# Decode attention: the last eight transposes of a set of cached latents are dealt out between the value matmuls of the preceding set

## The reference, cut to what matters

```python
def mla_sample(q_lat, q_rope, ckv_new, krope_new, cache_ckv, cache_krope, page_table):
    past_ckv = cache_ckv[page_table].reshape(Bd, -1, MLA_KV_LORA)      # (8, 4096, 256)
    past_kr = cache_krope[page_table].reshape(Bd, -1, MLA_ROPE)        # (8, 4096, 32)
    s_past = jnp.einsum('bthc,bsc->bhts', q_lat, past_ckv) + jnp.einsum('bthr,bsr->bhts', q_rope, past_kr)
    s_new = jnp.einsum('bthc,bsc->bhts', q_lat, ckv_new) + jnp.einsum('bthr,bsr->bhts', q_rope, krope_new)
    ...
    p = jax.nn.softmax(s, axis=-1).astype(ckv_new.dtype)
    return (jnp.einsum('bhts,bsc->bthc', p[..., :P], past_ckv) +
            jnp.einsum('bhts,bsc->bthc', p[..., P:], ckv_new))
```

## Time and profile before

| | |
|---|---|
| median of three executions | 1638.72 us (1634.9 to 1642.35) |
| the profiled execution, its own time | 1635.87 us |
| its span from first to last instruction | 1634.1 us |
| TensorE matmuls busy | 1535.8 us (94%) |
| VectorE busy | 933.1 us (57%) |
| ScalarE busy | 667.0 us (41%) |
| GpSimd busy | 165.0 us (10%) |
| mean granted clock of TensorE | 0.973 of full speed |

### The profile page before, as it was taken

One profiled execution on the slowest core, in us unless ns is written; L12 is line 12 of the kernel. 1 busy time (PEld: TensorE's weight loads), 2 busy tenths in 40 slices (PEclk: granted clock), 3 DMA queues, 4 the chain that ended last, 5 costly groups with the idle time before them and its releaser, 6 DMA issues.

```text
span 1634.1 us, 28976 instructions
## 1 busy us (share of the span) xinstructions
PE 1535.8 (94%) x11157; PEld 1287.6 (79%) x11157; DVE 933.1 (57%) x1761; ACT 667.0 (41%) x1283; POOL 165.0 (10%) x265
## 2 busy tenths in 40 slices
PE   6999998799999988798999999999999999999994
PEld 6989997556666655465888999999999998877683
DVE  6624303555455544455568777777777765454495
ACT  2246222633456633234123555555555543332341
POOL 2100000200000024330011000000000000000030
PEclk9999998999899989999999999999999999999997
DMA  7212111110000056654123122222222237645492
GB/s 252 88 54 65 44 53 44 42 52 14 27 1 27 2 219 211 202 184 166 65 90 105 58 75 76 78 78 78 78 78 78 78 110 272 186 148 186 147 302 86
DMA packets 108805, 171.50 MB, mean 105 GB/s; under 512 B 9786, under 2 KB 75192, under 8 KB 108680
## 3 DMA queue, kind: packets, MB, share of 16 engines
q1 hardware_dynamic: 93882, 117.74, 22.8%
q0 software_dynamic: 14688, 52.43, 9.3%
q10 hardware_dynamic: 144, 0.07, 0.0%
HBM read 142.59 MB, written 27.62 MB: 104 GB/s over the span
## 4 chain that ended last, share of the span: by engine, by line
PE 68%; DVE 3%; issue 2%; ACT 1%; another core or an unknown queue 1%; DMA 0%; POOL 0%; SPq 0%; ACTq 0%; DVEq 0%; POOLq 0%
PE ps L2236 9%; PE ps L2235 9%; PE ps L2234 9%; PE ps L210 7%; PE ps L211 7%; PE ps L212 7%; PE ps L1268 4%; PE ps L1598 4%; PE ps L1619 3%; PE ps L1305 2%; PE ps L1645 2%; PE ps L1282 2%; PE ps L2758 1%; DMA f_raw<-in_w_ffn_in 0%
## 5 line engine op out<-in xcount | busy, mean ns | idle before, releaser
L2234 PE MATMUL ps<-t_hi,op_hi 128*128 128x266 f32 (+1 forms) x672 | 191.6, 285 | 2.4 <-DVE gap_hi L2458 2.4
L2236 PE MATMUL ps<-t_hi,op_lo 128*128 128x266 f32 (+1 forms) x672 | 192.2, 286 | 0.0
L2235 PE MATMUL ps<-t_lo,op_hi 128*128 128x266 f32 (+1 forms) x672 | 192.0, 286 | 0.0
L210 PE MATMUL ps<-w_hi,hT_hi 128*128 128x256 f32 (+2 forms) x504 | 142.2, 282 | 3.4 <-DVE hT_lo L324 3.4
L2234 PE MATMUL ps<-h1T_hi,op_hi 128*128 128x266 f32 x504 | 143.4, 285 | 1.0 <-DVE gap_lo L2470 1.0
L2236 PE MATMUL ps<-h1T_hi,op_lo 128*128 128x266 f32 x504 | 144.1, 286 | 0.0
L2235 PE MATMUL ps<-h1T_lo,op_hi 128*128 128x266 f32 x504 | 143.4, 285 | 0.0
L210 PE MATMUL ps<-d_hi,g_hi 128*128 128x512 f32 x352 | 140.8, 400 | 1.2 <-issue 1.2
L212 PE MATMUL ps<-w_hi,hT_lo 128*128 128x256 f32 (+2 forms) x504 | 141.5, 281 | 0.0
L211 PE MATMUL ps<-w_lo,hT_hi 128*128 128x256 f32 (+2 forms) x504 | 141.4, 281 | 0.0
L211 PE MATMUL ps<-d_lo,g_hi 128*128 128x512 f32 x352 | 138.9, 395 | 0.0
(11 more groups left out here) (351 smaller groups left out, 3473.6 us busy)
## 6 DMA issues: line engine op xcount, KB each, us to landing
d_raw<-in_w_down SPq DMA_DIRECT2D x66, 512.0 KB, 3.6
f_raw<-in_w_ffn_in SPq DMA_DIRECT2D x88, 256.0 KB, 3.4
g_res<-gap_lo SPq DMA_DIRECT2D x22, 528.0 KB, 3.6
g_raw<-g_res SPq DMA_DIRECT2D x44, 192.0 KB, 3.9
w_raw<-in_w_in SPq DMA_DIRECT2D x6, 1024.0 KB, 5.3
xs<-in_x_prompt SPq DMA_DIRECT2D x8, 512.0 KB, 4.5
h_res<-xs POOLq DMA_DIRECT2D x8, 512.0 KB, 3.0
wo_raw<-in_w_o SPq DMA_DIRECT2D x2, 2048.0 KB, 7.5
```

The costliest lines, as they stand in the source:

```text
L210: nc.tensor.matmul(out, ah, bh, start=start, stop=False)
L2234: nc.tensor.matmul(o, ah, bh, start=FIRST_IN[q] and k == 0, stop=False, skip_group_check=again)
L2235: nc.tensor.matmul(o, ah, bl, start=False, stop=False, skip_group_check=again)
L2236: last = nc.tensor.matmul(o, al, bh, start=False, stop=k == 3, skip_group_check=again)
```

## The change

Only TensorE's list is changed. `turn_set`, which issued groups 0 to 5 or groups 6 to 8, becomes `turn_blocks`, which issues any run of single transposes. Groups 0 to 5 and group 6 stay where they were, before and after the transposes of the probabilities. The eight transposes of groups 7 and 8 go into `values`: behind each four value matmuls (one block j, all four sequences) come two of the eight. Where the preceding step is that of the new tokens (k = 1 and k = 10) there are only four value matmuls in all, and the eight transposes come behind them. In steps 9 and 18 nothing is transposed and nothing changes.

```diff
@@ -1584,19 +1584,22 @@
             wait_group_out(pe, pt_base[-1] - 1)
             pe.wait_ge(o_out, N_JOBS)
 
-            def turn_set(z, part):
+            def turn_blocks(z, first, count):
+
                 slot = z % SLOTS
-                if part == 0:
+                if first == 0:
                     pe.wait_ge(set_loaded[slot], 64 * (z // SLOTS + 1))
-                for n, t in turns(z)[0:SPLIT_TURN] if part == 0 else turns(z)[SPLIT_TURN:]:
-                    if t == 8:
+                for i in range(first, first + count):
+                    n, t = turns(z)[i // 4]
+                    j = i % 4
+                    if j == 0 and t == 8:
                         pe.wait_ge(rope_packed, z + 1)
-                    if n >= TURN_BANKS:
+                    if j == 0 and n >= TURN_BANKS:
                         wait_turn_out(pe, n - TURN_BANKS)
-                    for j in range(4):
-                        src = ring_c[slot][:, t // 2, j, P * (t % 2):P * (t % 2) + P] if t < 8 else ring_p[z % 2][:, j, :, :].rearrange("p b r -> p (b r)")
-                        last = nc.tensor.transpose(ps[:, n % TURN_BANKS, P * j:P * j + P], src, ident)
-                    last.then_inc(past_turned, 1)
+                    src = ring_c[slot][:, t // 2, j, P * (t % 2):P * (t % 2) + P] if t < 8 else ring_p[z % 2][:, j, :, :].rearrange("p b r -> p (b r)")
+                    last = nc.tensor.transpose(ps[:, n % TURN_BANKS, P * j:P * j + P], src, ident)
+                    if j == 3:
+                        last.then_inc(past_turned, 1)
 
             def scores(k):
                 g, s, z = s_steps[k]
@@ -1631,8 +1634,9 @@
                         last = nc.tensor.transpose(ps[:, 6, P * j:P * j + P], sprob[k % 2][:, P * j:P * j + P], ident)
                 last.then_inc(spt_turned, 1)
 
-            def values(k):
+            def values(k, turning):
                 g, s, z = s_steps[k]
+                left = 4 * (N_TURN - SPLIT_TURN) - 4
                 pe.wait_ge(spt_out, k + 1)
                 if k >= 1:
                     pe.wait_ge(sacc_done, k)
@@ -1644,18 +1648,23 @@
                             w, x = spt[k % 2][:, j, 32 * b:32 * b + 32], ring_c[z % SLOTS][:, b, j, :]
                         last = nc.tensor.matmul(ps[32 * b:32 * b + 32, 7, 0:KVL], w, x, start=j == 0,
                                                 stop=s is None or j == 3)
-                last.then_inc(spv_done, 1)
+                    if s is None or j == 3:
+                        last.then_inc(spv_done, 1)
+                    if turning is not None:
+                        m = left if s is None else left // 4
+                        turn_blocks(turning, 4 * SPLIT_TURN + 4 + m * j, m)
 
             n = len(s_steps)
             for k in range(n + 1):
-                if k < n and s_steps[k][1] is not None:
-                    turn_set(s_steps[k][2], 0)
+                turning = s_steps[k][2] if k < n and s_steps[k][1] is not None else None
+                if turning is not None:
+                    turn_blocks(turning, 0, 4 * SPLIT_TURN)
                 if k >= 1:
                     turn_probs(k - 1)
-                if k < n and s_steps[k][1] is not None:
-                    turn_set(s_steps[k][2], 1)
+                if turning is not None:
+                    turn_blocks(turning, 4 * SPLIT_TURN, 4)
                 if k >= 1:
-                    values(k - 1)
+                    values(k - 1, turning)
                 if k < n:
                     scores(k)
         def turn_latents(pe):
```

## The result

| | before | after |
|---|---|---|
| median | 1640.53 us (1634.9 to 1645.55, 4 runs) | 1672.53 us (1666.23 to 1677.52, 4 runs) |
| the profiled execution, its own time | 1635.87 us | 1666.23 us |
| its span | 1634.1 us | 1664.4 us |
| the stage, first scores of the new tokens to first matmul of the output projection | 188.6 us | 223.4 us |

The ratio of the times is 1.0194, with a 95% interval of 1.0144 to 1.0244: slower, by 32 us in the medians; whether by 2% or somewhat less the interval leaves open. The stage grew by 34.9 us; the rest of this one profiled execution was 4.6 us shorter, which is within the 11 us by which the runs of either kernel differ among themselves.

A forecast was written before the change was run, and what follows sets the result against it. The prediction took TensorE to bound the kernel: 14 steps x 2.83 = 39.6 us, less 1.4, 1.2 and 1.5, plus 2.1, gave +37.6 on 1635.87, thus 1673.5; it forecast a median of 1675 us, range 1656 to 1693.

The forecast's parts named there:

- Changes of shape: TensorE switching between transpose and value tile shapes: 0.28 us a round trip, four more per step, 1.13 us.
- the 0.16 that was borrowed: Going out from 128x32 values to whole-array transposes: 0.16 us, taken from the change from 32x32 to transposes.
- The first rival: Shape changes between values and transposes are free, transpose loads running under value passes: 1.82 us per step, 1661 us; chance 0.12.
- The new wait: Scores wait for VectorE's copy of group 8: start 1.06 us after the last transpose, 0.83 of it new.
- Values to scores: Stretch from first value matmul to scores in a regular step: from 1.75 to 4.58 us, 2.83 more, in 14 steps.
- What the first part gives back: Values start earlier with eight transposes fewer ahead: 0.48 us gained in three steps (1.4 in all), zero in eleven.
- the third rival: Lateness reaches the scores' notice: VectorE's maximum 1.4 us late in eleven steps, +15 us, 1690 us; chance 0.10.
- Single steps: Sets differing from the regular step: 4, 11, 12 together -1.2 us; set 5 -1.5; set 0 costs 1.1, set 8 1.0.
- The clock: Rival: TensorE's granted clock falls to 1.2 GHz for part of each step, 28 us more, 1703 us; chance 0.04.

## Why the prediction came out right, point by point

The forecast was 1675 us and the median is 1672.5; the stage grew by 34.9 us against 37.6. That the two medians lie so close is partly luck. The forecast counted from a median of 1638.72, and with the fourth execution that of before is 1640.53: the medians grew by 32.0 us, where the forecast meant 36.3. Its own sum would give 1676.3 (1635.87 + 37.6 + 2.85), and 1675 was written without a reason. Errors of the terms also went against each other; they are added up below the list. By the steps of the sum:

- **Changes of shape**: predicted 0.28 us a round trip, measured 0.285 and 0.29. Out of the values it is 0.57 us from the start of a run of eight passes to the first transpose and 0.36 from there back; the 0.16 that was borrowed from the change between two other shapes held. The first rival (free shapes, 0.65 us from run to run) is refuted by 0.94. The Trainium skill, "TensorEngine Tiling (Array Packing)", Key Properties, says that changing the tiling mode drains TensorE; these 0.29 us agree with it. The Trainium skill, "TensorE: Matmul & The Clock Gate", Part 2, says that the reorder window pulls weight loads ahead of matmuls in flight; across a change of shape the 0.94 us show no gain from it.
- **The new wait**: predicted 1.06 us from last transpose to scores and 0.83 new; measured 1.11 (the last transpose starts at 726.15, the scores at 727.26). Covered by other work it vanishes, and 0.88 us of the step with it. From copy to scores it takes 0.11, not the 0.06 read in set 0.
- **Values to scores**: predicted 4.58, measured 4.65 in 13 steps of the 14. With set 15 (5.82, passes at half speed at its start) and set 5 (its low clock gone, 3.41 to 4.65) the growth is 40.1 us against 39.6.
- **What the first part gives back**, 1.4 us in the sum: this is the term that was mis-sized. I took 0.48 us for three steps and zero for eleven. The amount was right (0.50 in the undisturbed steps), their number wrong: sets 6, 7 and 10 have gathers and lose nothing, and sets 2, 3 and 13 keep 0.15 to 0.18. I put the lateness on the copies of groups 0 to 2. It lands earlier: on the maximum of the scores (set 11: 0.45 after the first transpose, set 10: 0.14), and costs 0.3 us, not 0.5. Set 15, counted among the three, gained 2.06.
- **Late notice of the scores**, the third rival, thus came true as a mechanism and not in its size: the maximum begins 0.3 us late in eight steps (sets 2 to 5 and 11 to 14), where I priced 1.4 in eleven. With all eight transposes behind the values it was 1.2 us in four steps, which is the size I had feared.
- **Single steps**: sets 4, 11 and 12 lost their stall and gained 0.62 each ahead of the values (predicted -1.2 for the three beside no gain, measured -1.85 in all). Set 5 grew by 0.85, predicted 2.83 - 1.5 = 1.33. Set 0 grew by 1.09 (predicted 1.1), set 8 by 0.42 (predicted 1.0: its late copies absorbed more).
- **The clock**: no loss in the regular steps, and 0.94 over the stage before and after. Only set 15 shows slow passes among its values, 1.2 us in all: the granted clock is 0.51 from 788 to 790 us, after 2.04 us in which TensorE waited ahead of group 5.

Ahead of the values -7.4 us where 1.4, 1.2 and 1.5 were taken off, values to scores +40.1, scores to the next set +0.7, sets 0 and 8 +1.5: 34.9.

**Still open**: why notices of TensorE to ScalarE and VectorE come late while GpSimd's indirect gathers run, and what decides in which steps the lateness catches a notice that matters. In the changed kernel the sets with and without it have gathers at the same distance (3.7 us ahead of the first transpose in set 10 and in set 11).

## What to carry to other kernels

Putting matmuls of one kind between those of another can pay only where it fills a gap that is idle, or covers a wait. Here there was none, so each alternation between tiles 128x128 and 128x32 was a bare 0.29 us, and moving the last producer next to its consumer uncovered 0.88 us of a copy that independent work had hidden. Look behind the work you move for the wait it covers: the same eight transposes in one block behind the first values cost little more than a third of the change's price (ratio 1.0071 against 1.0194). And the price of an order counts only where that engine bounds: where page loads bound the stage, the same order cost 5 us instead of 32.

## What the runs showed of the hardware that I had not expected

While GpSimd issues indirect gathers, copies and maxima that wait for TensorE begin up to 1.6 us late with four gathers in a row (the copy of group 2 with one group less ahead of the probabilities begins 1.9 us after its last transpose instead of 0.3), and in set 5, with eight, `spt` begins 5.1 us late. In the six kernels without gathers, with plain transfers of the same bytes or with page-by-page loads no copy whose engine was idle began more than 0.53 us after its last transpose. With plain transfers the kernel before takes 34 us less of 1638; 20 of them lie in the stage, and the stage began 12 us sooner, for a reason that no run here separates.

Where the lateness falls moved with how far ahead of a step its gathers are released. With the first gather 2.3 us ahead of the first transpose (the kernel before) it holds the copy of group 2 or 3 until 3.4 us into the step; with 4.4 us ahead (all eight transposes behind the last values) it holds the maximum until 1.3 us into it, in both 5.7 us after that gather. With 3.7 us ahead, in the changed kernel, it held the maximum until 0.45 only, 4.2 us after the gather, so the 5.7 us are no rule. But a reordering shifts the gathers too, and with them the wait that they hit.
